# Gate/up matrices loaded whole, with rows of 16384 bytes, instead of in two halves

## The chip, the cores and the metric

The kernel runs on one core of one Trainium2 chip. The metric is the device time of one execution in microseconds (us), the median of several runs. The host only lays the arrays out.

## The reference, cut to what matters

One decoder layer for 264 tokens (256 of a prompt, 8 single new ones), width 1024: a gated short convolution and a complex-diagonal state-space mixer side by side, merged by gates, layer norm, then a mixture of experts, and layer norm again. The mixture is where the change lies:

```
scores = sigmoid(t @ w_router)                       # 64 experts
... group-limited top 8 of 64 per token, weights w normalised to 2.5
h = silu(einsum('td,edf->tef', t, w_gate)) * einsum('td,edf->tef', t, w_up)
routed = einsum('tef,efd->td', h * comb, w_down)
shared = (silu(t @ ws_gate) * (t @ ws_up)) @ ws_down
return routed + shared
```

Each expert has w_gate and w_up of 1024x256 and w_down of 256x1024, all f32. Gate and up of one expert lie side by side in one matrix of 128 partitions by 4096 numbers (2 MB); w_down is another MB, with rows of 8192 bytes. All 64 experts are read once.

## The kernel before, in words

**Front.** Ten products of width 1024 run as 80 strips (`strip`, L1111) of 512 KB each, loaded by SyncE through a ring of four slots (L370, rows of 4096 bytes). Between the late strips SyncE also loads the first experts' matrices by `load_gu` (L365) and the shared expert into slot 3, always halfway through the list `parts`.

**Experts.** They are taken in 32 pairs, one `visit` each. Slots for gate/up matrices are six (three pairs of slots, `SLOT_PAIRS`: (4,5), (0,1), (2,3)), for down matrices eight. A visit on TensorE does, in order: 32 gate/up matmuls (L1322; k from 0 to 7, the two experts side by side), the combine of the visit before (`combine`, L1295, 24 matmuls), two turns of h (L1335), eight turns of the gathered token rows of the next visit (`turn`, L1270, which waits for that gather), the selection of a later pair, and 16 down matmuls (L1359). In the last six visits one chunk of the shared expert's down product comes in too (L1300). The gather itself is an indirect DMA that GpSimd issues (L484) once TensorE has finished the previous turn and VectorE the index list; it brings up to 128 rows of 4096 bytes into x_rows.

**Loads of the experts.** SyncE alone issues them, in program order, and its queue is one. `refill(it)` loads for visit it + 3 into the slots that visit it gives back. A gate/up matrix is moved as two halves of 1 MB (k 0 to 3, then k 4 to 7), each with rows of 8192 bytes and a semaphore of its own. TensorE raises `gu_mid` after k = 3 and `gu_done` after k = 7; SyncE waits for `gu_mid`, issues the first halves of both slots, waits for `gu_done`, issues the second halves, waits for `dn_done` and issues the two down matrices. On the other side TensorE waits for the first halves before k = 0 and for the second before k = 4. Slot 3 first holds the shared expert; its first half is refilled once `shared_mid` is raised and the first gather has landed (L403), its second after all shared gate/up products.

Of the kernel before, what the change touches and what calls it, by code (L numbers as in the profile page):

```python
# [28 lines left out]
HC = KC // 2  # L29
E = 64  # L30
F = 256
# [55 lines left out]
def build(nc, x_t, w_front, vecs, b_sm, c_sm, h0, conv_state, w_router, w_gu, w_dn,  # L87
          o_y, o_conv_p, o_conv_s, o_ssm_p, o_ssm_s):
    with ExitStack() as ctx:
# [3 lines left out]
        def sem(name):  # L93
            return ctx.enter_context(nc.semaphore(name))
# [75 lines left out]
        gu = [gu_ring[:, i] for i in range(SLOTS)] + [gu_4, gu_5]  # L170
# [91 lines left out]
        iotas_ready = sem("iotas_ready")  # L262
        gathers_cleared = sem("gathers_cleared")
        shared_gu = sem("shared_gu")
        shared_mid = sem("shared_gu_first_halves")
        shared_silu = sem("shared_silu")
        shared_h = sem("shared_h")
        shared_dn = sem("shared_dn")
        shared_used = sem("shared_used")
        gu_in = [[sem(f"gu_slot{i}_half{h}_loaded") for h in range(2)] for i in range(6)]  # L270
        dn_in = [sem(f"dn_slot{i}_loaded") for i in range(8)]
        dve_idx = sem("dve_idx")
        shifted = sem("positions_shifted")
# [3 lines left out]
        gathered = [sem(f"gathered{i}") for i in range(2)]  # L277
        turned = sem("turned")
        xg_ready = sem("xg_ready")
        gu_mid = sem("gu_first_half_done")  # L280
        gu_done = sem("gu_done")
        silu_done = sem("silu_done")
        hx_ready = sem("hx_ready")
# [43 lines left out]
        with nc.Block() as block:  # L327
# [17 lines left out]
            def _(sp):  # L345
# [13 lines left out]
                sp.dma_start(cst[:], conv_state).then_inc(s_cst, 16)  # L359
                sp.dma_start(cS, c_sm).then_inc(s_c, 16)  # L360

                def load_gu(s, w, halves=range(2)):

                    for h in halves:
                        sp.dma_start(gu[s][:, HC * h:HC * h + HC], w[:, HC * 2 * F * h:HC * 2 * F * (h + 1)]).then_inc(gu_in[s][h], 16)  # L365

                parts = [("gu", 2, 0), ("dn", 2, 0), ("gu", 3, 1), ("dn", 3, 1), ("gu", 0, 4), ("dn", 4, 2), ("gu", 4, 2), ("dn", 5, 3), ("gu", E, 3), ("dn", E, 6)]
                for n in range(RING, STRIPS):
# [13 lines left out]
                    if n > GLU + 2 and n % 2 == 0 and parts:  # L382
                        kind, e, s = parts.pop(0)
# [15 lines left out]
                    sp.wait_ge(xrow_ready, c + 1)  # L399
                    sp.dma_start(x_dram[c * P:c * P + tok[c]], xrow[c][0:tok[c]]).then_inc(rows_stored, 16)  # L400

                sp.wait_ge(shared_mid, 1)
                sp.wait_ge(gathered[0], 16)  # L403
                load_gu(3, w_gu[5], [0])
                sp.wait_ge(shared_gu, 2 * FC)
                load_gu(3, w_gu[5], [1])

                def refill(it, slots, downs, experts):

                    for h, through in enumerate((gu_mid, gu_done)):  # L410
                        sp.wait_ge(through, it + 1)
                        for s, e in zip(slots, experts):
                            sp.dma_start(gu[s][:, HC * h:HC * h + HC], w_gu[bass.ds(e, 1), :, HC * 2 * F * h:HC * 2 * F * (h + 1)].rearrange("o p f -> (o p) f")).then_inc(gu_in[s][h], 16)
                    sp.wait_ge(dn_done, it + 1)
                    for s, e in zip(downs, experts):
                        if s is not None:
                            sp.dma_start(dn[s], w_dn[bass.ds(e, 1)].rearrange("o p f -> (o p) f")).then_inc(dn_in[s], 16)
# [679 lines left out]
            def _(pe):  # L1097
# [55 lines left out]
                for n in range(US, CG):  # L1153
                    if n == TURN_AT:
                        pe.wait_ge(bb_ready, 1)
                        for r in range(2):
                            for c in range(KC):
                                ins = pe.transpose(psum[:, 2 * r + c // 4, (c % 4) * P:(c % 4) * P + P],
                                                   bb[:, r, PB * c:PB * c + PB].rearrange("p t c -> p (t c)"), ident[:])
# [45 lines left out]
                for k in range(KC):  # L1205
                    for half in range(2):
                        ins = pe.matmul(psum[E * half:E * half + E, 1, 0:1], wr[:, k], vec[:, V_LN + KC + k:V_LN + KC + k + 1], start=(k == 0), stop=(k == KC - 1))
# [3 lines left out]
                for k in range(KC):  # L1211
                    for half, tokens in enumerate((slice(0, HT), slice(P, T))):
                        ins = pe.matmul(psum[E * half:E * half + E, 0, 0:HT], wr_g[:, k], r_[:, k, tokens], start=(k == 0), stop=(k == KC - 1))
                ins.then_inc(logits_ready, 1)

                def turn_scores():
                    pe.wait_ge(scores_ready, 1)
                    for c, (half, at) in enumerate(((0, 0), (1, 0), (1, P))):
                        rows = slice(E * half, E * half + E)
                        ins = pe.transpose(scores_in[:, c], scores_t[rows, at:at + P], ident[rows, rows])  # L1220
                    ins.then_inc(scores_turned, 1)

                def shared_in(f, first, end):
                    for k in range(first, end):
                        ins = pe.matmul(psum[:, SHARED_BANKS[f], 0:T], gu[3][:, k, f * P:f * P + P], x1[:, k], start=(k == 0), stop=(k == KC - 1))  # L1225
                    if end == KC:
                        ins.then_inc(shared_gu, 1)
                    return ins

                def turn_x1(c, k):  # L1230
                    return pe.transpose(psum[0:tok[c], 2 * (c % 2) + k // 4, (k % 4) * P:(k % 4) * P + P], x1[:, k, c * P:c * P + tok[c]], ident[:])
# [1 line left out]

                keep_warm(6, 2)
                turn_scores()
                for h in range(2):
                    pe.wait_ge(gu_in[3][h], 16)
                for k in range(KC):
                    pe.wait_ge(x1_ready, k + 1)
                    for c in range(2):  # L1240
                        ins = turn_x1(c, k)
# [5 lines left out]
                for k in range(KC):  # L1247
                    ins = turn_x1(2, k)
# [3 lines left out]
                for c in range(TC + 1):  # L1252
                    for b in range(min(c + 1, TC)):
                        ins = pe.matmul(psum[:, 6, c * E:c * E + E], tri16[:] if b == c else ones16[:], pk[:, b], start=(b == 0), stop=(b == min(c, TC - 1)))
# [19 lines left out]
                pe.wait_ge(select_ready, 1)  # L1274
                select_part(0, 1, selected)
                pe.wait_ge(xrow_ready, TC)
                shared_in(3, 0, HC).then_inc(shared_mid, 1)
                pe.wait_ge(select_ready, 2)
                pe.wait_ge(idx_ready, 1)
                select_part(1, 1, selected)  # L1280
# [22 lines left out]
                def combine(u, first, shared):  # L1303

                    for n in range(KC):
                        if n >= SUMS:

                            pe.wait_ge(added, first + (n - SUMS + 2))
                        if n == shared:
                            pe.wait_ge(dn_in[6], 16)  # L1310
                            shared_down(n, SUM_BANKS[n % SUMS])
                        combine_chunk(n, u, SUM_BANKS[n % SUMS], shared=(n == shared))

                def visit(it, u, slots, downs, loaded, first_down=None, before=None, gathers=None, shared=None):


                    pe.wait_ge(xg_ready, it + 1)
                    for k in range(KC):
                        for j in range(2):
                            if k % HC == 0:  # L1320
                                pe.wait_ge(gu_in[slots[j]][k // HC], loaded + (16 if slots[j] == 3 else 0))
                            ins = pe.matmul(psum[SL * j:SL * j + SL, GU_BANK, :], xg[:, k, SL * j:SL * j + SL], gu[slots[j]][:, k],  # L1322
                                            start=(k == 0), stop=(k == KC - 1))
                        if k == HC - 1:
                            ins.then_inc(gu_mid, 1)
                    ins.then_inc(gu_done, 1)

                    if before is not None:
                        pe.wait_ge(y_split, it)
                        pe.wait_ge(sw_ready, it)  # L1330
                        combine(1 - u, before, shared)

                    pe.wait_ge(hx_ready, it + 1)
                    for f in range(FC):
                        ins = pe.transpose(psum[:, GU_BANK, f * P:f * P + P], h_sl[:, f * P:f * P + P], ident[:])  # L1335
                    ins.then_inc(h_turned, 1)

                    if gathers is not None:
                        pe.wait_ge(gathered[1 - u], gathers)
                        turn()  # L1340

                        pe.wait_ge(select_ready, it + 3)
                        pe.wait_ge(idx_ready, it + 2)
                        pe.wait_ge(weights_read, 4)
                        select(u, (it + 2) % PAIRS)

                    if before is None:
                        pe.wait_ge(shared_h, FC)
                    if gathers is None:
                        shared_down(0, LAST_BANKS[0], alone=True).then_inc(shared_first, 1)  # L1350
                    for j in range(2):
                        pe.wait_ge(dn_in[downs[j]], loaded if downs[j] != 4 and downs[j] != 7 else first_down)
                    pe.wait_ge(hT_ready, it + 1)
                    if before is not None:
                        pe.wait_ge(added, before + (KC + 1))
                    for h in range(2):
                        for f in range(FC):
                            for j in range(2):
                                ins = pe.matmul(psum[SL * j:SL * j + SL, 4 + h, :], hT_sl[:, f, SL * j:SL * j + SL],  # L1359
                                                dn[downs[j]][:, f, h * 512:h * 512 + 512], start=(f == 0), stop=(f == FC - 1))  # L1360
                        if gathers is None:
                            ins.then_inc(last_dn, 1)
                    if gathers is not None:
                        ins.then_inc(dn_done, 1)
# [126 lines left out]
```

## Time and profile before

| | us |
|---|---|
| median of 3 runs | 849.26 (848.98 to 850.16) |
| span of the profiled execution | 847.7 |
| TensorE busy | 830.9 (98%) |
| VectorE busy | 472.2 (56%) |
| chain that ended last: on TensorE | 94% of the span |
| data moved | 262.06 MB, mean 309 GB/s |

The page gives no time of its own for the profiled execution, only its span, which runs from the first to the last instruction; the median lies 1.6 us above it. Busy shares are averages over stages. The front lasts to about 327 us, routing to about 359, the 32 visits to about 828, the last layer norm to the end.

### The profile page before, as it was taken

The numbers are of one execution on the slowest core, as the hardware profiler recorded it, in microseconds if no ns is written. First come the engines' busy times: TensorE is split into PE (matmuls) and PEld (weight loads), VectorE is DVE, ScalarE is ACT, GpSimd is POOL, SyncE is SP. The second block draws the span as 40 slices with busy tenths as digits, with TensorE's granted clock in tenths as the row PEclk, the third lists the DMA queues.
The fourth block names the chain that finished last, engine by engine and source line by source line (L and its number), as shares of the span: only waits on it lengthen the run. The fifth ranks groups of instructions, "written<-read, shape, count | busy, mean of one in ns | idle before, by whom it ended". The sixth has DMA issues, their size and how long they took to land.

```text
span 847.7 us, 12937 instructions
## 1 busy us (share of the span) xinstructions
PE 830.9 (98%) x4681; PEld 513.8 (61%) x4681; DVE 472.2 (56%) x1174; ACT 190.4 (22%) x281; POOL 84.1 (10%) x89
## 2 busy tenths in 40 slices
PE   8999999999999999899999999999999999999995
PEld 7876788777888887644444545454544444454553
DVE  6979899889111215734545555454545454554557
ACT  2210111001100004423222222222232322222224
POOL 1029800000010000100000000000000000000000
PEclk9999999999999999999999999999999999999998
DMA  9443344333689985599999999999999999999951
GB/s 332 143 138 103 109 147 148 123 100 107 152 298 348 379 309 199 180 359 412 419 421 418 421 419 421 420 420 421 419 420 421 420 421 419 419 420 419 420 248 52
DMA packets 50550, 262.06 MB, mean 309 GB/s; under 512 B 10504, under 2 KB 11272, under 8 KB 25296
## 3 DMA queue, kind: packets, MB, share of 16 engines
q1 hardware_dynamic: 45904, 252.88, 75.5%
q0 software_dynamic: 4608, 8.66, 2.8%
q8 instruction: 26, 0.43, 0.2%
q14 instruction: 12, 0.10, 0.0%
HBM read 267.10 MB, written 2.53 MB: 318 GB/s over the span
## 4 chain that ended last, share of the span: by engine, by line
PE 94%; DVE 4%; DMA 1%; ACT 0%; issue 0%; SPq 0%; ACTq 0%; DVEq 0%
PE banks L1111 34%; PE banks L1322 26%; PE banks L1359 13%; PE banks L1295 10%; PE banks L1270 3%; PE banks L1126 1%; PE banks L1139 1%; PE banks L1185 1%; PE banks L1300 1%; PE banks L1335 1%; PE banks L1142 1%; PE banks L1225 1%; DMA ring<-w_front 1%; DVE xT L1081 0%; PE banks L1383 0%
## 5 line engine op out<-in xcount | busy, mean ns | idle before, releaser
L1322 PE MATMUL banks<-high,low 128*64 128x512 f32 x848 | 225.2, 592 | 0.1
L1111 PE MATMUL banks<-xT,ring 128*128 128x264 f32 x768 | 178.2, 390 | 0.9 <-DMA ring<-w_front 0.9
L1111 PEld LDWEIGHTS banks<-xT,ring 128*128 128x128 f32 x768 | 143.7, 190 | 33.8 <-issue 8.8
L1322 PEld LDWEIGHTS banks<-high,low 128*64 128x64 f32 x848 | 73.3, 137 | 143.7 <-issue 142.7
L1029 DVE TENSOR_TENSOR cgb<-cgb,banks 128x264 f32<-128x264 f32 x256 | 93.4, 422 | 51.9 <-PE banks L1295 51.5
L1063 DVE SCALAR_TENSOR_TENSOR high<-banks,sml,low 128x1024 f32<-128x1024 f32 x31 | 39.8, 1284 | 124.2 <-ACT low L608 124.2
L1295 PE MATMUL banks<-xT,low 128*128 128x264 bf16 x744 | 92.6, 277 | 0.1
L1295 PEld LDWEIGHTS banks<-xT,low 128*128 128x128 bf16 x744 | 66.0, 98 | 42.7 <-issue 25.2
L1322 PE MATMUL banks<-ring,low 128*64 128x512 f32 x176 | 77.5, 593 | 0.0
L1359 PE MATMUL banks<-high,mu 128*64 128x512 f32 x336 | 76.7, 598 | 0.0
L484 POOL DMA_INDIRECT low<-x_rows_dram,idx x32 | 32.0, 998 | 435.1 <-DVE idx L976 430.8
L1066 DVE TENSOR_TENSOR low<-high,low 128x1024 bf16<-128x1024 f32 x31 | 38.0, 1225 | 37.0 <-ACT low L610 37.0
L608 ACT ACTIVATE low<-banks,sml 128x1024 bf16<-128x1024 f32 x31 | 34.5, 1114 | 81.5 <-PE banks L1359 81.5
L1359 PEld LDWEIGHTS banks<-high,mu 128*64 128x64 f32 x336 | 22.2, 136 | 36.8 <-issue 36.3
L610 ACT ACTIVATE low<-high 128x1024 bf16<-128x1024 f32 x31 | 32.7, 1056 | 41.9 <-DVE high L1063 41.9
L1359 PE MATMUL banks<-us,mu 128*64 128x512 f32 x88 | 40.1, 598 | 0.0
L785 DVE TENSOR_TENSOR_SCAN high<-high 128x2112 f32<-128x2112 f32 x8 | 36.8, 4647 | 3.8 <-POOL high L450 3.7
L576 ACT ACTIVATE low<-banks 128x1024 f32<-128x1024 f32 x32 | 32.8, 1025 | 23.2 <-PE banks L1270 23.2
L593 ACT ACTIVATE mu<-banks 128x256 f32<-128x256 f32 x32 | 12.3, 384 | 108.9 <-PE banks L1322 108.9
L1270 PE MATMUL banks<-ident,low 128*128 128x128 f32 x256 | 33.2, 273 | 0.0
L596 ACT ACTIVATE mu<-banks 128x256 f32<-128x256 f32 x32 | 12.3, 384 | 91.0 <-PE banks L1335 91.0
L1111 PE MATMUL banks<-bgb,ring 128*128 128x264 f32 x128 | 29.6, 386 | 0.0
(273 smaller groups left out, 899.1 us busy)
## 6 DMA issues: line engine op xcount, KB each, us to landing
high<-w_gu SPq DMA_DIRECT2D x108, 1024.0 KB, 23.8
high<-w_dn SPq DMA_DIRECT2D x42, 1024.0 KB, 23.3
ring<-w_front SPq DMA_DIRECT2D x78, 512.0 KB, 3.2
ring<-w_gu SPq DMA_DIRECT2D x22, 1024.0 KB, 25.3
us<-w_dn SPq DMA_DIRECT2D x11, 1024.0 KB, 23.8
bgb<-w_dn SPq DMA_DIRECT2D x6, 1024.0 KB, 21.6
xcb<-w_dn SPq DMA_DIRECT2D x5, 1024.0 KB, 21.8
xT<-x_t SPq DMA_DIRECT2D x4, 264.0 KB, 3.8
```

The lines of the kernel that those rows point to most:

```text
L576: act.activation(xg.rearrange("p (b k) s -> p b (k s)", b=2), psum[:, 2:4], ACT.Copy).then_inc(xg_ready, 1)
L608: act.activation(y_terms[:, 0], psum[:, 4:6].rearrange("p b f -> p (b f)"), ACT.Copy, scale=gain[:, u]).then_inc(first_term, 1)
L610: act.activation(y_terms[:, 1], y_rest, ACT.Copy).then_inc(second_term, 1)
L785: st.did(dve.tensor_tensor_scan(seg, decay.rearrange("p t c -> p (t c)"), seg, 0.0, ALU.mult, ALU.add))
L1029: dve.tensor_tensor(acc[:, n], acc[:, n], psum[:, bank, 0:T], ALU.add).then_inc(added, 1)
L1063: dve.scalar_tensor_tensor(y_rest, psum[:, 4:6].rearrange("p b f -> p (b f)"), gain[:, u], y_terms[:, 0], ALU.mult, ALU.subtract).then_inc ...
L1066: dve.tensor_tensor(y_terms[:, 2], y_rest, y_terms[:, 1], ALU.subtract).then_inc(y_split, 1)
L1111: ins = pe.matmul(psum[:, 6 + n % 2, 0:T], ring[:, n % RING, k], rhs[:, k], start=(k == 0), stop=(k == KC - 1))
L1270: ins = pe.transpose(psum[:, 2 + k // 4, (k % 4) * P:(k % 4) * P + P], x_rows[:, k * P:k * P + P], ident[:])
L1295: ins = pe.matmul(psum[:, bank, 0:T], y_terms[:, term, n * P:n * P + P], sw[:, u], start=(term == 0 and not shared), stop=(term == 2))
L1322: ins = pe.matmul(psum[SL * j:SL * j + SL, GU_BANK, :], xg[:, k, SL * j:SL * j + SL], gu[slots[j]][:, k], start=(k == 0), stop=(k == KC - 1))
L1359: ins = pe.matmul(psum[SL * j:SL * j + SL, 4 + h, :], hT_sl[:, f, SL * j:SL * j + SL], dn[downs[j]][:, f, h * 512:h * 512 + 512], start=(f ...
```

## The change

Every gate/up matrix is one transfer of 2 MB with rows of 16384 bytes and one semaphore. SyncE waits only for `gu_done` before it refills both slots; `gu_mid` and `shared_mid` are gone. TensorE waits for the whole matrix of each slot before that slot's k = 0. The refill of slot 3 is issued whole where its second half was. Bytes, order of slots, arithmetic and buffers are the same.

```
-        gu_in = [[sem(f"gu_slot{i}_half{h}_loaded") for h in range(2)] for i in range(6)]
+        gu_in = [sem(f"gu_slot{i}_loaded") for i in range(6)]
...
-                def load_gu(s, w, halves=range(2)):
-
-                    for h in halves:
-                        sp.dma_start(gu[s][:, HC * h:HC * h + HC], w[:, HC * 2 * F * h:HC * 2 * F * (h + 1)]).then_inc(gu_in[s][h], 16)
+                def load_gu(s, w):
+
+                    sp.dma_start(gu[s], w).then_inc(gu_in[s], 16)
...
-                sp.wait_ge(shared_mid, 1)
                 sp.wait_ge(gathered[0], 16)
-                load_gu(3, w_gu[5], [0])
                 sp.wait_ge(shared_gu, 2 * FC)
-                load_gu(3, w_gu[5], [1])
+                load_gu(3, w_gu[5])
...
-                    for h, through in enumerate((gu_mid, gu_done)):
-                        sp.wait_ge(through, it + 1)
-                        for s, e in zip(slots, experts):
-                            sp.dma_start(gu[s][:, HC * h:HC * h + HC], w_gu[bass.ds(e, 1), :, HC * 2 * F * h:HC * 2 * F * (h + 1)].rearrange("o p f -> (o p) f")).then_inc(gu_in[s][h], 16)
+                    sp.wait_ge(gu_done, it + 1)
+                    for s, e in zip(slots, experts):
+                        sp.dma_start(gu[s], w_gu[bass.ds(e, 1)].rearrange("o p f -> (o p) f")).then_inc(gu_in[s], 16)
...
-                            if k % HC == 0:
-                                pe.wait_ge(gu_in[slots[j]][k // HC], loaded + (16 if slots[j] == 3 else 0))
+                            if k == 0:
+                                pe.wait_ge(gu_in[slots[j]], loaded + (16 if slots[j] == 3 else 0))
...
-                        if k == HC - 1:
-                            ins.then_inc(gu_mid, 1)
```

## Rows read from the trace of the kernel before

**Rows 1.** Chain that ended last, one visit: start us, us, what.
```profile
516.96 6.87 PE banks L1322 x32
523.83 2.90 PE banks L1295 x24
526.94 0.87 PE banks L1270 x8
527.87 3.58 PE banks L1359 x16
531.46 6.87 PE banks L1322 x32
```

**Rows 2.** Waits, whole span: us in total, times, longest us.
```profile
PEld banks L1111 <- DMA ring<-w_front: 1.9, 3, 1.3
```

**Rows 3.** Busy time by stretch: us, engines, TensorE clock, DMA share, GB/s.
```profile
400.00:500.00 100.00, 100.00 (x591) 46.97 (x589) 50.72 (x133) 27.75 (x35) 5.94 (x6) 1.00 1.02 420
775.00:800.00 25.00, 25.00 (x149) 12.65 (x148) 10.71 (x29) 7.54 (x9) 1.98 (x2) 1.00 1.02 420
818.00:820.00 2.00, 2.00 (x16) 1.06 (x12) 0.43 (x1) 0.38 (x1) 0.00 (x0) 1.00 0.17 70
```

**Rows 4.** DMA packets of 10:20, 278:285, 330:335 and 400:500, in this order.
```profile
DMA packets 1051, 4.16 MB, mean 416 GB/s; under 512 B 112, under 2 KB 240, under 8 KB 795
...
DMA packets 561, 2.82 MB, mean 403 GB/s; under 512 B 60, under 2 KB 60, under 8 KB 374
...
DMA packets 291, 2.12 MB, mean 424 GB/s; under 512 B 32, under 2 KB 32, under 8 KB 32
...
DMA packets 6505, 41.99 MB, mean 420 GB/s; under 512 B 1147, under 2 KB 1147, under 8 KB 1618
```

**Rows 5.** SyncE's queue as the refills begin: start us, us.
```profile
355.00 4.21 SPq L365 DMA_DIRECT2D high<-w_gu  x2
...
366.16 0.33 SPq L413 DMA_DIRECT2D high<-w_gu  x1
```

**Rows 6.** Single issues at 355.0, 366.5, 770.1, 786.8 and 790.7: us to landing.
```profile
high<-w_gu SPq DMA_DIRECT2D x1, 1024.0 KB, 4.9
...
ring<-w_gu SPq DMA_DIRECT2D x1, 1024.0 KB, 10.9
...
ring<-w_gu SPq DMA_DIRECT2D x1, 1024.0 KB, 29.6
...
high<-w_gu SPq DMA_DIRECT2D x1, 1024.0 KB, 28.5
...
high<-w_dn SPq DMA_DIRECT2D x1, 1024.0 KB, 29.4
```

**Rows 7.** SyncE's queue, last refills.
```profile
770.11 5.11 SPq L413 DMA_DIRECT2D ring<-w_gu  x1
...
786.83 1.99 SPq L413 DMA_DIRECT2D high<-w_gu  x1
```

**Rows 8.** TensorE in visits 30 and 31.
```profile
796.24 0.59 PE L1322 MATMUL banks<-high,low 128*64 128x512 f32 x1
...
799.67 0.59 PE L1322 MATMUL banks<-high,low 128*64 128x512 f32 x1
799.76 0.64 PE L1322 MATMUL banks<-ring,low 128*64 128x512 f32 x1
...
811.85 7.16 PE L1322 MATMUL banks<-high,low 128*64 128x512 f32 x32
```

**Rows 9.** Gathers: all 32 issues, one issue, and the turn it feeds.
```profile
DMA to landing us min/median/max: 3.7/8.1/9.4
...
370.08 0.99 POOL L484 DMA_INDIRECT low<-x_rows_dram,idx  x1 [12.25 <-DVE idx L976]
...
381.82 1.04 PE L1270 MATMUL banks<-ident,low 128*128 128x128 f32 x8
```

**Rows 10.** Strip loads L370: us to landing.
```profile
DMA to landing us min/median/max: 3.0/3.2/9.8
```

More of the change, by code:

```diff
@@ L264, in build @@
         shared_gu = sem("shared_gu")
-        shared_mid = sem("shared_gu_first_halves")
         shared_silu = sem("shared_silu")
@@ L279, in build @@
         xg_ready = sem("xg_ready")
-        gu_mid = sem("gu_first_half_done")
         gu_done = sem("gu_done")
@@ L1235, in _ @@
                 turn_scores()
-                for h in range(2):
-                    pe.wait_ge(gu_in[3][h], 16)
+                pe.wait_ge(gu_in[3], 16)
                 for k in range(KC):
@@ L1276, in _ @@
                 pe.wait_ge(xrow_ready, TC)
-                shared_in(3, 0, HC).then_inc(shared_mid, 1)
+                shared_in(3, 0, HC)
                 pe.wait_ge(select_ready, 2)
```

## The prediction

> **What bounds the kernel now.** I read the chain of waits first. In the visits it is TensorE back to back: 6.87 us of gate/up matmuls, 2.90 of combine, 0.87 of turns, 3.58 of down matmuls, and the next visit starts 14.50 us after the last, with no wait between [rows 1]. The list of waits has one entry of any size for TensorE against a load, 1.9 us in the strips [rows 2]. So far a kernel bound by TensorE, in which loads are hidden and their form is worth nothing.
>
> The table by stretch says otherwise. From 400 to 500 us and from 775 to 800 the DMA engines are busy for all of the time (share 1.02) at 420 GB/s, beside a TensorE that is also always busy [rows 3]. A visit needs 6 transfers of 1 MB, 6.29 million bytes, and its gather, some 0.27 million (66 rows of 4096 bytes of the 128 that are asked for; the rest is out of bounds). At 420 GB/s that is 15.6 us, against 14.5 on TensorE. The engines fall about 1.1 us per visit further behind, and the three pairs that were loaded early pay for it. The question is whether the credit lasts to the end, and it does, by nothing: the last second half for visit 30 was issued at 770.11 and took 29.6 us, so it landed at 799.7 [rows 6, 7], and TensorE, which took up the visit at 796.24, reached k = 4 at 799.67; its matmul from that slot starts at 799.76 and is stretched, 0.64 us for 0.59 [rows 8]. For visit 31 the last half landed at 786.83 + 28.5 = 815.3, the visit began at 811.85 and k = 4 is due 3.43 us later, at 815.28; its 32 matmuls span 7.16 us instead of 7.04. The last down matrix landed at 790.7 + 29.4 = 820.1, some 4 us before its use. After 818 the engines are nearly idle (share 0.17) [rows 3]. So both are bounds at once in the last three visits, and TensorE alone before.
>
> **The change part by part.**
>
> *Waits before k = 4 and the increment at k = 3 go.* The matmul pairs follow each other every 0.43 us with no gap there, so this gives nothing until visit 30, and some 0.1 us in each of the last two.
>
> *The whole matrix is due at k = 0.* That moves the due time of the second halves 3.43 us forward (4 of 8 steps of 0.43 twice over: 799.67 - 796.24). The arrival of the last byte of the pair doesn't move by it, since the same four megabytes come in one run either way. Where loads are early this costs nothing; at the end it decides: visit 30 would wait 799.7 - 796.24 = 3.5 us, visit 31 815.3 - 811.85 = 3.5 us. These are not added: once visit 30 is 3.5 late, visit 31 is late by as much and finds its matrices just landed.
>
> *Refills are issued later.* The stream of loads has to be followed from its start. Now 1 MB goes out at 355.0, 1 MB near 358.9, two after k = 3 of visit 0, two from 366.16; the very last of these was issued at 366.5 and landed at 366.5 + 10.9 = 377.4 [rows 5, 6]. In the changed kernel slot 3 goes out whole at 358.9 and four megabytes at 366.2. A lone MB took 4.9 us to land, of which its bytes are 2.6 (6.56 MB in 15.6 us), so 2.3 is the delay before them. Slot 3 then lands at 358.9 + 2.3 + 5.2 = 366.4, the engines have nothing until about 368.5, and the four megabytes land by 366.2 + 2.3 + 4 x 2.6 = 378.9. The stream is 1.5 us late. From there on the engines never ran dry before, and the next issues (372.0, 378.9) still come before the queue is empty, so 1.5 stays. Bounds: 0, if the gap is filled by what overlaps, to 2.4 (the gap and the MB that no longer flows at 355, counted whole). Later the time of issue doesn't matter: SyncE itself is held up at the end (5.11 us for an issue of 0.33 [rows 5, 7]) because the queue is full, 28 us deep.
>
> *Rows of 16384 bytes.* What a packet costs beside its bytes isn't shown for rows this long; it follows from stretches in which the engines were full, with time = packets x a + bytes x b over 16 engines. 10:20 (160 us of engine time, 1051 packets, 4.16 MB, mostly rows of 4096) against 330:335 (80 us, 291 packets, 2.12 MB, nearly all 8192) gives a = 0.006 us [rows 4]. 10:20 against 400:500 gives 0.004. 278:285 against 330:335 gives 0.03, though that stretch may not be full. A MB of gate/up saves 4 row packets per engine and half a completion, 4.5 x a. With a = 0.006 it is 0.027 us per MB, 0.11 us per visit, and over the 29 pairs refilled before visit 31 it is 3.1 us; with 0.004 it is 2.1; with 0.03 it is 15; and 0 or a small loss if the engines cut long rows up or like them less. I take 2.6, between the two stretches that were surely full.
>
> The Trainium skill ("DMA: Bandwidth & Descriptors", section "Why small descriptors are slow") puts a fixed 3 cycles on each packet beside one per 32 bytes; a row of 8192 is 256 beats, so by an estimate from that page doubling the row saves 0.6% of the gate/up time, or 1.8 us by the end. The trace agrees in size.
>
> *SyncE issues 60 transfers fewer*, at 0.33 to 0.43 us each, and none of it is on a path: it waits for TensorE or for the queue.
>
> *Front.* A strip load is issued three strips (10.7 us) ahead and lands in 3.2 us, at most 9.8 [rows 10]; the same bytes stand ahead of it in the queue as before. Cost nothing; gain at most the 1.9 us of [rows 2], which fall mostly at the very start, where no such matrix is loaded.
>
> *Sum.* Last landing for visit 31: 815.3 + 1.5 (late start) - 2.6 (longer rows) = 814.2. TensorE could start it at 811.85 - 0.1, so it starts 2.4 us late; k = 4 no longer stumbles, 0.1 back. Visit 30 gives the same: 799.7 + 1.5 - 2.5 - 796.24 = 2.5. What follows is unchanged, since the down matrices (820.1 - 1.1 = 819.0) are early. The end moves by +2.3 us: 847.7 + 2.3 = 850.0 of span, and with the 1.6 us by which the median lies above the span of the profiled execution, 851.6.
>
> **Rivals.**
>
> *The gathers become late (slower by more).* A gather takes 3.7 us to land when the engines are idle and 8.1 (at most 9.4) beside 8192-byte rows [rows 9]. The extra 4.4 us is what its packets lose by taking turns with SyncE's queue. If each turn lasts as long as one row, it is twice that beside gate/up rows: 12.5 us when only they flow, about 3.7 + 4.4 x 5/3 = 11.0 on the average of a visit. The room is 381.82 - 370.08 = 11.74 us. So a third of the visits would wait up to 0.8 us at the turn, and TensorE has nothing else to do: some 10 x 0.4 = 4 us, up to 30 x 0.8 = 24 if all are hit or the 9.4 is the rule. Up to 2 or 3 us it hides in the landing wait above; beyond, it adds. Time: 853 to 873, the middle 856. For it: the extra was the same in nearly all 30 gathers. Against: what takes turns may be smaller than a row.
>
> The Trainium skill ("DMA: Bandwidth & Descriptors", section "Queues, rings and completion order") says that an engine changes queues only at packet boundaries, with 9 to 17 descriptors typical in a packet. By that rule a turn is a whole transfer's share and doubles as well, from 2.6 to 5.2 us: the same 12.5 us at worst, and the same time.
>
> *The longer rows pay for all (not slower).* If a is 0.011 us or more, 29 x 4 x 4.5 x a is 5.7 us and the last pair is whole at k = 0. TensorE is then never kept waiting and the end moves by -0.3 to 0: 849.0 to 849.3. It decides at 0.0095 (a gain of 5.0). For it: the 0.03 of one stretch. Against: the two full ones. It can't go further down, as TensorE's own chain stands and has no wait to lose.
>
> *The rows are cut up.* If packets stay at 8192 bytes, the gain is nil and the end moves by 1.5 + 3.4 = +4.9: 854.2.
>
> **How the numbers follow.** Within 0.2% (1.7 us) no change can be told from this kernel's scatter. Landing wait of 0.5 to 5 us, cut-up rows included: 0.52, of which 0.15 below 1.7 us. Late gathers: 0.15. Long rows pay for all: 0.27. Faster by something that no row shows: 0.06. Slower 0.37 + 0.15 = 0.52, same 0.27 + 0.15 = 0.42, faster 0.06. The likeliest gives 851.6; its own range is 849.8 to 854.3. The range of 8 in 10 takes in the case of no wait below and most of the gather's above: 848.8 to 858.0.
>
> **What would show it.** Right: 16384-byte packets (some 8300 packets fewer), GB/s of the stretch 400 to 500 at 421 to 425; TensorE waiting for w_gu at the first matmul of the last two or three visits, 2 to 3 us in all, and none earlier; visits of 14.5 us before. The last load landing within 2 us of 820. Wrong: waits at L1270 for the gather; waits for w_gu in visits below 25; no waits at all; an unchanged packet count; a stream of loads whose rate falls under 418.

## The result, and the profile after

The changed kernel takes 851.01 us (median, 850.59 to 852.11) against 849.25 for the kernel before beside it: ratio 1.0022 (95% interval 1.0015 to 1.0029), 1.8 us slower. In a later comparison on another chip it was 851.69 against 849.20, ratio 1.0025 (1.0016 to 1.0035). The forecast was 851.6.

The profiled execution took 851.09 us, with a span of 849.3. Its chain of waits now names a load (the first line is the chain by engine, the second the chain by line):

```profile
PE 90%; DMA 4%; DVE 4%; ACT 0%; issue 0%; POOL 0%; SPq 0%; ACTq 0%; DVEq 0%; POOLq 0%
PE banks L1105 34%; PE banks L1315 24%; PE banks L1350 12%; PE banks L1288 9%; DMA high<-w_gu 4%; PE banks L1263 3%; PE banks L1120 1%; PE banks L1133 1%; PE banks L1179 1%; PE banks L1293 1%; PE banks L1136 1%; PE banks L1326 1%; PE banks L1219 1%; PE banks L1143 0%; DVE xT L1075 0%
```

L1315 is the gate/up matmul (L1322 before), L1350 the down matmul; SyncE issues its refills at L407. The chain in order of time shows the place (start us, us, what); it answers to [rows 1]:

```profile
683.65 36.78 DMA high<-w_gu
720.44 0.04 issue
720.48 7.08 PE banks L1315 x30
...
728.89 2.38 PE banks L1288 x21
...
736.01 7.16 PE banks L1315 x32
...
751.60 7.12 PE banks L1315 x32
```

A gate/up matrix of 2 MB, issued at 683.65, landed at 720.44. TensorE had taken up visit 25 at 719.32 with the matrix of the other slot, and its queue stood until this one was there. That is the first wait in the visits: all from visit 1 to 24 last 14.5 us, as before. Visit 25 took 16.5 us to the next start (735.84) where it took 15.3 before, and three more lose 0.3 us each:

| start of visit, from visit 1 | before | changed | more |
|---|---|---|---|
| 25 | 347.90 | 347.90 | 0.0 |
| 26 | 363.21 | 364.42 | 1.2 |
| 27 | 378.51 | 380.01 | 1.5 |
| 28 | 393.80 | 395.56 | 1.8 |
| 29 | 409.10 | 410.87 | 1.8 |
| 30 | 424.40 | 426.47 | 2.1 |
| 31 | 440.01 | 441.95 | 1.9 |

(The starts are those of the first gate/up matmul in the two timelines: visit 1 at 371.84 and 371.42, visit 25 at 719.74 and 719.32, visit 31 at 811.85 and 813.37.)

The DMA engines' rate, which answers to [rows 3] and [rows 4] (busy time by stretch, then packets of 400 to 500 us):

```profile
400.00:500.00 100.00, 100.00 (x591) 46.98 (x589) 50.72 (x133) 27.75 (x35) 5.95 (x6) 1.00 1.01 424
816.00:818.00 2.00, 2.00 (x12) 1.26 (x10) 0.81 (x2) 1.06 (x1) 0.00 (x0) 1.00 0.12 49
```

```profile
DMA packets 4661, 42.36 MB, mean 424 GB/s; under 512 B 944, under 2 KB 944, under 8 KB 1415
```

424 GB/s for 420, with 1844 packets fewer (9360 fewer in the whole span, 41190 for 50550), so the long rows did travel as packets of 16384 bytes. From 816 to 818 the engines are nearly idle (share 0.12, before 0.74), and the last load lands at 818.4 where it landed at 820.2. Faster loads, an earlier end of them, and yet a later end of the kernel.

The start of the refills, which answers to [rows 5] and [rows 6] (SyncE's queue, then the issues at 358.5, 366.1 and 378.9 with the time to landing):

```profile
358.53 0.37 SPq L362 DMA_DIRECT2D high<-w_gu  x1
365.74 0.34 SPq L407 DMA_DIRECT2D high<-w_gu  x1
366.11 0.43 SPq L407 DMA_DIRECT2D ring<-w_gu  x1
```

```profile
high<-w_gu SPq DMA_DIRECT2D x1, 2048.0 KB, 8.7
...
ring<-w_gu SPq DMA_DIRECT2D x1, 2048.0 KB, 12.7
...
high<-w_gu SPq DMA_DIRECT2D x1, 2048.0 KB, 14.7
```

The first pair's four megabytes land at 366.1 + 12.7 = 378.8 (worked out as 378.9), the next four at 378.9 + 14.7 = 393.6. By the same working, with the megabyte of the down matrix that was issued between them, they would have landed at 378.9 + 5 x 2.6 = 391.9.

The gathers, which answer to [rows 9] (least, median and most us to landing):

```profile
DMA to landing us min/median/max: 3.3/10.4/11.4
```

The median is 2.3 us more than before, and the longest is still inside the 11.74 us that there are.

### The profile page after: what moved, and what is told of

It is laid out like the page before. It is cut to its first block, busy times and chain, and to the rows that moved or that the text cites. A ratio compares the mean times of both kernels' runs of the same rounds, so it can differ in the third digit from the quotient of the medians.

```text
span 849.3 us, 12776 instructions
## 1 busy us (share of the span) xinstructions
PE 833.4 (98%) x4681; PEld 520.9 (61%) x4681; DVE 472.3 (56%) x1174; ACT 190.3 (22%) x281; POOL 84.8 (10%) x89
## 2 busy tenths in 40 slices
DMA packets 41190, 262.06 MB, mean 309 GB/s; under 512 B 9464, under 2 KB 10232, under 8 KB 24256
## 4 chain that ended last, share of the span: by engine, by line
PE 90%; DMA 4%; DVE 4%; ACT 0%; issue 0%; POOL 0%; SPq 0%; ACTq 0%; DVEq 0%; POOLq 0%
PE banks L1105 34%; PE banks L1315 24%; PE banks L1350 12%; PE banks L1288 9%; DMA high<-w_gu 4%; PE banks L1263 3%; PE banks L1120 1%; PE banks L1133 1%; PE banks L1179 1%; PE banks L1293 1%; PE banks L1136 1%; PE banks L1326 1%; PE banks L1219 1%; PE banks L1143 0%; DVE xT L1075 0%
## 5 line engine op out<-in xcount | busy, mean ns | idle before, releaser
L1315 PE MATMUL banks<-high,low 128*64 128x512 f32 x848 | 227.0, 592 | 0.3
L1315 PEld LDWEIGHTS banks<-high,low 128*64 128x64 f32 x848 | 78.3, 137 | 137.4 <-issue 133.2
L1315 PE MATMUL banks<-ring,low 128*64 128x512 f32 x176 | 77.4, 593 | 0.0
L1350 PE MATMUL banks<-high,mu 128*64 128x512 f32 x336 | 76.7, 598 | 0.0
L1350 PEld LDWEIGHTS banks<-high,mu 128*64 128x64 f32 x336 | 22.2, 136 | 36.8 <-issue 36.3
L1350 PE MATMUL banks<-us,mu 128*64 128x512 f32 x88 | 40.1, 598 | 0.0
L570 ACT ACTIVATE low<-banks 128x1024 f32<-128x1024 f32 x32 | 32.8, 1024 | 23.4 <-PE banks L1263 23.4
```

The costliest lines, as they stand in the source:

```text
L570: act.activation(xg.rearrange("p (b k) s -> p b (k s)", b=2), psum[:, 2:4], ACT.Copy).then_inc(xg_ready, 1)
```

## The experiments

All times are medians beside the kernel before in the same job: 849.20 us for e1 to e4, 849.51 for e5 to e7, 849.20 for e8 to e10. The expectations name two theories. By the landing theory TensorE is late by as much as the last load lands after it is due. By the packet theory each packet costs its DMA engine a fixed time beside that of its bytes.

**e1: late issue alone.**

```
-                sp.wait_ge(shared_mid, 1)
                 sp.wait_ge(gathered[0], 16)
-                load_gu(3, w_gu[5], [0])
                 sp.wait_ge(shared_gu, 2 * FC)
-                load_gu(3, w_gu[5], [1])
+                load_gu(3, w_gu[5])
...
-                    for h, through in enumerate((gu_mid, gu_done)):
-                        sp.wait_ge(through, it + 1)
+                    sp.wait_ge(gu_done, it + 1)
+                    for h in range(2):
```

> Kernel before, but both halves of a pair are refilled at gu_done, and both of slot 3 after the shared products. Rows of 8192, TensorE still waits by halves. Landing theory: the stream of loads starts 1.1 to 1.5 us late, so the last second half of visit 31 lands at 816.4 to 816.8 in place of 815.3, due at 815.3: +1.1 to +1.5 us, median 850.4 to 850.8. Rival (the queue is full anyway, so the time of issue costs nothing): 849.3.

Measured 851.38, ratio 1.0028 (1.0019 to 1.0038), +2.2 us (1.6 to 3.2). The rival is out; the cost is above what was expected. From visit 1 to visit 31 it takes 442.02 us for 440.01.

**e2: the whole matrix due at k = 0, alone.**

```
-                            if k % HC == 0:
-                                pe.wait_ge(gu_in[slots[j]][k // HC], loaded + (16 if slots[j] == 3 else 0))
+                            if k == 0:
+                                for h in range(2):
+                                    pe.wait_ge(gu_in[slots[j]][h], loaded + (16 if slots[j] == 3 else 0))
```

> Kernel before, but TensorE waits for both halves of both slots before k = 0; loads and their issue as before. Landing theory: the last half lands as before at 815.3 and is due at 811.8: +3.4 us, median 852.6, with TensorE waiting for a load in visit 25 already (last half at 721.3, start 719.7). Rival (the due time is hidden by the credit of early loads): 849.3.

Measured 851.92, ratio 1.0037 (1.0024 to 1.0050), +2.7 us (2.0 to 4.2). The visits start at 719.42 (25) and 735.81 (26), so the first loss is in visit 25, as expected.

**e3 and e10: both, with rows of 8192.** Both edits above in one kernel; e10 is the same kernel in a job with the changed one (e9).

> Both of the other two edits together: the changed kernel in all but the rows, which stay at 8192 bytes in transfers of 1 MB. Landing theory: the two costs add, +4.5 to +4.9 us, median 853.8 to 854.2, and the difference to the changed kernel's 851.0 (2.8 to 3.2 us) is what the longer rows give. Rival (longer rows give nothing, the costs are smaller than worked out): 851.0. Gathers land in 8.1 us, not in the 10.4 of the changed kernel.

> The changed kernel on the same chip as the next one, so that the worth of the longer rows can be read from one job: 851.0.

> The changed kernel with rows of 8192 bytes, again. It stood at 855.6 in the first job, 4.6 us above the changed kernel of another job, where the packets of the trace (0.0076 us each, 4.5 per MB and engine, 116 MB) give 4.0 us. Packet theory: 3.5 to 4.5 us above the changed kernel here. Rival (the forecast's 2.6): 853.6.

Measured e3 855.58, ratio 1.0075 (1.0062 to 1.0088); e10 855.79, ratio 1.0072 (1.0059 to 1.0086); e9 851.69. So the two costs together are 6.4 to 6.6 us, more than expected, and the long rows give 855.79 - 851.69 = 4.1 us back. By the two intervals that is some 2.7 to 5.5 us: the 4.0 of the packet theory fits well, and the forecast's 2.6 lies just below. The waits begin earlier than in the changed kernel: visit 24 starts 15.7 us after visit 23 (690.35 to 706.09). The gathers land in 8.1 us.

**e4: the changed kernel with the old times for its first loads.** Slot 3 and the first pair come by halves again, all later pairs whole.

```
-                    sp.wait_ge(gu_done, it + 1)
-                    for s, e in zip(slots, experts):
-                        sp.dma_start(gu[s], ...)
+                    if downs[0] is None:
+                        for h, through in enumerate((gu_mid, gu_done)):
+                            sp.wait_ge(through, 1)
+                            for s, e in zip(slots, experts):
+                                half(s, e, h)
+                    else:
+                        ...
```

> Changed kernel, but the refill of slot 3 and the first pair's refill go by halves at the old times (after the first shared halves, after k = 3, after k = 7); all later ones whole with rows of 16384. Landing theory: the stream is 1.1 to 1.5 us earlier, median 849.5 to 849.9, the waits for w_gu at visits 25 and on nearly gone. Rival (the late start is made up in the full queue): 851.0.

Measured 850.18, ratio 1.0011 (1.0002 to 1.0019): 0.8 us below the changed kernel's 851.0 of another job, less than the 1.1 to 1.5. Visit 31 begins 440.6 us after visit 1, so 0.6 of the 1.9 us is left. The table by stretch shows where the rest is:

```profile
378.00:380.00 2.00, 2.00 (x17) 1.25 (x14) 0.81 (x3) 0.38 (x1) 0.00 (x0) 1.00 0.65 127
380.00:382.00 2.00, 2.00 (x19) 1.58 (x18) 2.00 (x7) 0.20 (x1) 0.00 (x0) 1.00 0.60 238
```

The DMA engines finish the first pair earlier and then run out, since visit 1's refill still waits for its last matmul (378.5). The changed kernel had 410 and 385 GB/s there. The gap is partly moved on, not closed.

**e5: rows of 4096.** The kernel before with each half in two transfers of 512 KB.

```
+                            for c in (2 * h, 2 * h + 1):
+                                sp.dma_start(gu[s][:, 2 * c:2 * c + 2], w_gu[bass.ds(e, 1), :, 4 * F * c:4 * F * (c + 1)]...).then_inc(gu_in[s][h], 16)
```

> Kernel before, each half moved as two quarters of 512 KB with rows of 4096 bytes, issued at the same times, waited for by halves. Packet theory (0.0076 us per packet and engine, from the packets of 400 to 500 us before and after the change): 9 packets more per MB and engine, 0.27 us per visit, the last load for visit 31 8 us later: median 857, rate in the full stretch 412 to 413 GB/s. Rival (rows cost nothing beyond their bytes, the 424 against 420 has another cause): 849.3 and 420 GB/s. Gathers, if a turn at an engine lasts as long as a row or a transfer: about 6.6 us in place of 8.1.

Measured 857.16, ratio 1.0090 (1.0076 to 1.0105), with this line for 400 to 500 us:

```profile
DMA packets 10047, 41.20 MB, mean 412 GB/s; under 512 B 1542, under 2 KB 1542, under 8 KB 8502
```

Time and rate as the packet theory had them. The expectation for the gathers missed: the median is 7.6 us, not 6.6.

**e6: rows of 16384 in transfers of 1 MB.** The changed kernel, each matrix split by partitions.

```
+                        for h in range(2):
+                            sp.dma_start(gu[s][64 * h:64 * h + 64], w_gu[bass.ds(e, 1), 64 * h:64 * h + 64]...).then_inc(gu_in[s], 16)
```

> Changed kernel, each matrix in two transfers of 1 MB by partitions (0 to 63, 64 to 127), rows still 16384 bytes. If a gather's turn lasts as long as a row: gathers land in 10.4 us as in the changed kernel. If it lasts as long as a transfer's share: 8.1. Time 851.0 by the packet theory (one completion more per MB, +0.5 us at most), if 64 partitions spread over the engines as 128 do; much more, with GB/s well under 420, if they don't.

Measured 1296.45 us (1255.15 to 1330.34). It could not answer its question, because loads over 64 partitions didn't run at the rate of those over 128, and the gathers took 18.8 us (median):

```profile
400.00:500.00 100.00, 79.38 (x412) 37.01 (x412) 35.32 (x94) 19.42 (x24) 4.94 (x5) 0.88 1.01 243
600.00:700.00 100.00, 55.64 (x248) 21.64 (x247) 20.58 (x54) 11.89 (x15) 2.97 (x3) 0.74 1.01 208
```

**e7: the floor.** The changed kernel with half of each down matrix left unloaded in the refills.

```
-                            sp.dma_start(dn[s], w_dn[bass.ds(e, 1)]...)
+                            sp.dma_start(dn[s][:, 0], w_dn[bass.ds(e, 1), :, 0:D]...)
```

> Changed kernel, but each down refill brings only the first of its two rows of 4096 bytes per partition, so half the bytes and wrong expert outputs. 5 MB a visit take 13 us, less than TensorE's 14.5: by the landing theory all waits for w_gu go and the median is the floor of TensorE's chain, 848.9 to 849.3. Rival (something else in the changed kernel slows TensorE, the gathers above all): about 851.

Measured 849.11, ratio 0.9996 (0.9987 to 1.0004). With the loads lightened nothing is left of the change's cost, and the kernel before already stood at TensorE's floor within that interval. The gathers are faster here too (8.5 us), so this run alone doesn't clear them. The changed kernel's own trace does: its visits 1 to 24 take 14.5 us each, with gathers of up to 11.4 us.

**e8: transfers of 2 MB with rows of 8192.** The kernel before, with the halves of two neighbouring slots in one transfer, for two of the three pairs of slots.

```
+                        if slots[0] < SLOTS:
+                            s, e = slots[0], experts[0]
+                            sp.dma_start(gu_ring[:, s:s + 2, HC * h:HC * h + HC]..., w_gu[bass.ds(e, 2), :, ...]...).then_inc(gu_in[s][h], 16)
+                            continue
```

> Kernel before, but for the slot pairs (0,1) and (2,3) the first halves of both slots come as one transfer of 2 MB, the second halves as another; rows stay 8192 bytes, times of issue and due times as before. If a gather is slowed by the length of a row, it lands in 8.1 us as before; if by the size of a transfer, in about 10 us as in the changed kernel. If what raised the rate to 424 GB/s is longer rows, it stays at 420 and the median at 849.3 to 849.8; if it is fewer completions, it rises by a quarter or so of the 4 GB/s.

Measured 849.15, ratio 0.9997 (0.9988 to 1.0006). The first line is the stretch 400 to 500, the second its packets, the third all gathers:

```profile
400.00:500.00 100.00, 100.00 (x591) 47.01 (x589) 50.76 (x133) 27.75 (x35) 5.95 (x6) 1.00 1.01 419
...
DMA packets 6356, 41.93 MB, mean 419 GB/s; under 512 B 1006, under 2 KB 1006, under 8 KB 1477
...
DMA to landing us min/median/max: 3.8/8.1/9.6
```

Neither the rate nor the gathers changed. From 400 to 500 us there are 141 packets under 512 B fewer than before (1006 for 1147), where the changed kernel has 203 fewer (944), and the rate didn't rise at all. So it is the length of a row that raises the rate and slows the gathers, not the size or the number of the transfers. The time couldn't have shown it: the kernel before has next to no wait left to lose.

## Why the prediction was right, and where its terms were off

**The mechanism held.** In its last visits the kernel was bound by TensorE and by its loads at once, a visit's loads outlasting the visit; the credit of the early loads ran out at the end. The step "the whole matrix is due at k = 0" and the step "refills are issued later" each cost time alone (e2, e1), and the longer rows paid for most of it (e10 against e9). e7, and the undisturbed visits 1 to 24, show that nothing else was in play. Of the signs named beforehand, the packets (9360 fewer), the rate (424 GB/s), the size of the wait (1.9 to 2.2 us, for 2 to 3) and the last landing (818.4) came; the place of the first wait did not.

| term | forecast, us | measured, us | by |
|---|---|---|---|
| late start of the stream | +1.5 | +2.2 | e1 |
| whole matrix due at k = 0 | +3.4 | +2.7 | e2 |
| both together | +4.9 | +6.4, +6.6 | e3, e10 |
| rows of 16384 bytes | -2.6 | -4.1 | e9, e10 |
| sum | +2.3 | +1.8, +2.5 | the changed kernel, e9 |

**Two sizes and the place of the waits were off. That the two sizes nearly cancelled, some 1.6 us more cost against 1.5 us more gain, was luck.**

*The sum of the two costs.* Both together exceed the sum of e1 and e2 by 1.5 to 1.7 us, which lies within the intervals of e1 and e2. The traces say more than the medians. The table counts from the start of visit 1, in the profiled executions:

| | last gate/up landing | start of visit 31 |
|---|---|---|
| before | 443.5 | 440.0 |
| late issue alone (e1) | 445.6 | 442.0 |
| whole matrix due, alone (e2) | 442.9 | 442.5 |
| both, rows of 8192 (e3) | 445.6 | 445.2 |
| both, rows of 8192 (e10) | 446.5 | 446.2 |
| changed | 442.1 | 442.0 |
| changed (e9) | 442.4 | 442.2 |

The due time moves by 3.4 us in each of e2, e3 and e10, as worked out. What differs is the landing: 0.6 us earlier than before in e2 (3.4 - 0.6 = 2.8), 2.1 later in e3 (5.5), 3.0 later in e10 (6.5), though e3 and e10 are the same kernel. So the term for the due time had its right size, and no joint effect is needed; why the last landing differs by 0.9 us between two executions of one kernel stays open.

*The late start was too small.* The step said that the engines never ran dry again before and that 1.5 us stays; by the landings it is 2.1 (e1, e3) to 3.0 (e10). The first pair landed to 0.1 us as worked out, the second 1.7 us later than worked out. From the profiles of the two kernels, the bytes moved from 354 to 410 us sum to 20.9 MB before and 20.3 MB in e1 (the table by stretch, rate times length), 0.65 MB or 1.6 us behind, while e1's visit 1 begins 0.5 us earlier: 2.1 us in all, and e1 loses 2.0 between visits 1 and 31. The step's premise was wrong as well. In the profiled execution of the kernel before the engines did run partly dry a second time, just after the first pair:

```profile
378.00:380.00 2.00, 2.00 (x17) 1.05 (x12) 0.58 (x2) 0.38 (x1) 0.00 (x0) 1.00 0.77 307
```

From 374 to 382 us that execution moved 356 GB/s; e2 and e8, which issue these loads at the same times, moved 423 and 420. So the 1.5 us was counted from a stream that itself stumbled there.

*The rows' gain was too small.* The step took a, the cost of a packet beside its bytes, from stretches of the trace before (0.004 and 0.006 us), none of which had rows of 16384. Worked from 400 to 500 us of both kernels, 1844 packets fewer made room for 0.37 MB, 14 us of the 1600 us of engine time: a = 0.0076 us. From 8192 down to 4096 (e5) it is 0.0085. The difference between the two is that of a short stretch: from 400 to 700 us the same working gives 0.0085 and 0.0086 (packets before, changed and e5):

```profile
DMA packets 19536, 126.05 MB, mean 420 GB/s; under 512 B 3450, under 2 KB 3450, under 8 KB 4857
...
DMA packets 14104, 127.26 MB, mean 424 GB/s; under 512 B 2849, under 2 KB 2849, under 8 KB 4256
...
DMA packets 29927, 123.70 MB, mean 412 GB/s; under 512 B 4608, under 2 KB 4608, under 8 KB 25057
```

With 0.0085 the gain is 29 x 4 x 4.5 x 0.0085 = 4.4 us, with 0.0076 it is 4.0. The Trainium skill's 3 cycles per packet ("DMA: Bandwidth & Descriptors", section "Why small descriptors are slow") would by an estimate be 0.6% of the gate/up time, 1.8 us. The 4.1 measured is more than twice that, so the measurement decides against it as the whole cost of a packet.

*Where the waits would be was wrong.* The text expected them in the last two or three visits and none earlier; the first and largest is in visit 25, seven visits from the end. The landing theory had it in the trace before: the last half for visit 25 was issued at 694.3 and took 27.1 us (its row):

```profile
high<-w_gu SPq DMA_DIRECT2D x1, 1024.0 KB, 27.1
```

It landed at 721.4, where the visit began at 719.74: already 1.7 us late for k = 0. From visit 25 on (seven visits, not the six named at the start) a visit has four extra matmuls of the shared expert and lasts 15.3 us, nearly the 15.5 of its loads (6.56 MB at 424 GB/s), so the shortfall hardly grows there. The working looked at the last visits alone.

**The rivals.** *The gathers become late* was closer than its chance: median 10.4 us (11.0 worked out), worst 11.4, room 11.74, and no visit waited. Its assumption was only half right. Beside the loads of the changed kernel they range from 8.3 to 11.4 us, longer on the whole where gate/up rows are more of the traffic. Rows of 4096, 8192 and 16384 go with some 6.8 (the shorter ones of e5), 8.1 and about 10.5 us: some 0.3 us per 1024 bytes of row on a base of 5.6, an estimate from these three, where the rival scaled all 4.4 us above the idle 3.7. The Trainium skill ("DMA: Bandwidth & Descriptors", section "Queues, rings and completion order") has an engine change queues only at packet boundaries, with 9 to 17 descriptors typical in a packet. Read as a whole transfer's share per turn this isn't borne out: with transfers of 2 MB and rows of 8192 (e8) the gathers still take 8.1 us. *The longer rows pay for all* needed a = 0.0095 for costs of 4.9 us. At 0.0076 to 0.0085 they paid for 4.1 of 6.6, so against the measured costs even 0.0095 (5.0 us) would not have been enough. *The rows are cut up* is out by the packet count.

## What to carry to other kernels

When an engine and the DMA queue are both full, look for the visit in which the last byte lands nearest to its first use, by landing times; a chain of waits that is all TensorE hides it. Merging two halves into one transfer costs the lead of the second half at both ends (it is asked for later and due earlier); the longer rows repay that only by the packets they save. Count the steps of the stage in which the credit is spent, not only its last ones: where a step of the stage grows longer, the shortfall stops growing.

## What the runs showed of the hardware

- A packet cost about 0.0085 us of its DMA engine beside its bytes, from 400 to 700 us, both between rows of 16384 and 8192 and between 8192 and 4096: full rates of 424, 420 and 412 GB/s for traffic whose gate/up rows have these lengths.
- A gather beside a full queue took longer with longer rows in the other queue (8.1 us beside 8192 bytes, 10.4 in the changed kernel) and not with larger transfers (8.1 in e8).
- SyncE's queue held more bytes in fewer, longer rows: by issues and landings 9 to 12 MB late in the visits before, 12 to 16 in the changed kernel. Before, issues of 0.33 us grew to 5.11 [rows 7] with 27 to 30 us of loads outstanding. In the changed kernel the gate/up loads issued after 683 us stood 32 to 39 us in the queue, and their issues took 0.33 to 0.4 us but for three of 1.6, 2.7 and 2.4. That would fit a limit counted in rows rather than bytes, which wasn't tested.
- Loads over 64 partitions with rows of 16384 moved 243 GB/s from 400 to 500 us and about 208 later, with the DMA engines as busy as at 424 (share 1.01). The granted TensorE clock of that stretch was 0.88, then 0.74, while TensorE was busy for 79% and 56% of the time.
